# Two blocks in float32 on one core: a convolution's steps moved by one slot, a quarter of x turned before the first group

## The reference

```python
h = _rmsnorm(x, norm_pre_w[l])
proj = jnp.einsum('bsd,de->bse', h, w_in[l])
(q, k, v, o_g, z_a, i_pre, f_pre, u_b, z_b, g_a, g_b) = _partition(proj)
qk = jax.nn.silu(_causal_depthwise_conv(jnp.concatenate([q, k], axis=-1),
                                        qk_conv_w[l], qk_conv_b[l]))
```

## Time and profile before

| | us |
|---|---|
| three timed runs: lowest, median, highest | 1443.83, 1444.13, 1444.65 |
| profiled execution, its own time | 1438.61 |
| its span, first to last instruction | 1436.9 |
| PE busy in the span | 1424.9 |
| DVE busy | 879.3 |
| ACT busy | 702.4 |
| mean granted clock of PE | 0.999 |

### The profile page before, as it was taken

One profiled execution on the slowest core, in us unless ns is written; L12 is line 12 of the kernel. 1 busy time (PEld: TensorE's weight loads), 2 busy tenths in 40 slices (PEclk: granted clock), 3 DMA queues, 4 the chain that ended last, 5 costly groups with the idle time before them and its releaser, 6 DMA issues.

```text
span 1436.9 us, 27127 instructions
## 1 busy us (share of the span) xinstructions
PE 1424.9 (99%) x10514; PEld 1347.1 (94%) x10514; DVE 879.3 (61%) x1071; ACT 702.4 (49%) x925; POOL 67.7 (5%) x99
## 2 busy tenths in 40 slices
PE   8999999999999999999999999999999999999997
PEld 8999988899999999999999999888999998888886
DVE  5778774546766777546464655557555545667754
ACT  6555545445555433434334444436433345777643
POOL 1000000001010100000000000001000002211000
PEclk9999999999999999999999999999999999999999
DMA  7565555655556556565666666756655554334653
GB/s 273 188 208 179 195 182 178 208 181 179 160 176 197 181 173 193 173 198 183 204 193 193 195 194 222 246 180 219 201 169 174 176 179 130 117 118 149 220 194 126
DMA packets 72658, 265.98 MB, mean 185 GB/s; under 512 B 8168, under 2 KB 8432, under 8 KB 71664
## 3 DMA queue, kind: packets, MB, share of 16 engines
q1 hardware_dynamic: 70704, 253.38, 54.6%
q0 software_dynamic: 1440, 10.63, 2.0%
q10 hardware_dynamic: 432, 0.79, 0.2%
HBM read 260.56 MB, written 4.20 MB: 184 GB/s over the span
## 4 chain that ended last, share of the span: by engine, by line
PE 97%; DMA 1%; issue 0%; DVE 0%; SPq 0%; ACT 0%; POOL 0%; ACTq 0%; POOLq 0%; DVEq 0%
PE ps L370 21%; PE ps L374 21%; PE ps L372 21%; PE ps L362 9%; PE ps L364 9%; PE ps L363 9%; PE ps L489 2%; PE ps L792 1%; PE ps L581 1%; PE ps L592 1%; DMA raw<-in_w_stream 1%; PE ps L630 0%; PE ps L798 0%; PE ps L796 0%; SPq L463 0%
## 5 line engine op out<-in xcount | busy, mean ns | idle before, releaser
L1271 DVE TENSOR_TENSOR wl<-raw,wh 128x1024 fp32r<-128x1024 f32 x474 | 580.5, 1231 | 482.6 <-ACT wh L957 470.7
L957 ACT ACTIVATE wh<-raw 128x1024 fp32r<-128x1024 f32 x474 | 497.8, 1058 | 521.4 <-PE ps L374 376.0
L370 PE MATMUL ps<-xh,wh 128*128 128x256 f32 x1568 | 436.0, 278 | 0.5 <-DVE xl L1280 0.3
L372 PE MATMUL ps<-xl,wh 128*128 128x256 f32 x1568 | 434.0, 277 | 0.0
L374 PE MATMUL ps<-xh,wl 128*128 128x256 f32 x1568 | 434.0, 277 | 0.0
L370 PEld LDWEIGHTS ps<-xh,wh 128*128 128x128 f32 x1568 | 294.5, 188 | 1.2 <-DVE xl L1280 0.9
L372 PEld LDWEIGHTS ps<-xl,wh 128*128 128x128 f32 x1568 | 294.7, 188 | 0.1
L374 PEld LDWEIGHTS ps<-xh,wl 128*128 128x128 f32 x1568 | 294.6, 188 | 0.0
L370 PE MATMUL ps<-x2h,wh 128*128 128x272 f32 (+1 forms) x432 | 123.8, 287 | 0.0
L374 PE MATMUL ps<-x2h,wl 128*128 128x272 f32 (+1 forms) x432 | 123.3, 286 | 0.0
L372 PE MATMUL ps<-x2l,wh 128*128 128x272 f32 (+1 forms) x432 | 122.9, 285 | 0.0
(11 more groups left out here) (370 smaller groups left out, 2292.1 us busy)
## 6 DMA issues: line engine op xcount, KB each, us to landing
raw<-in_w_stream SPq DMA_DIRECT2D x474, 512.0 KB, 4.1
xr<-in_x POOLq DMA_DIRECT2D x1, 2048.0 KB, 13.1
x_kept<-xr POOLq DMA_DIRECT2D x1, 2048.0 KB, 8.1
x1r<-x_kept POOLq DMA_DIRECT2D x1, 2048.0 KB, 9.5
xn<-in_x SPq DMA_DIRECT2D x7, 256.0 KB, 7.1
out<-yn SPq DMA_DIRECT2D x6, 256.0 KB, 3.5
mrow<-bound_rows POOLq DMA_DIRECT2D x8, 128.0 KB, 3.6
poolw<-in_pool_w POOLq DMA_DIRECT2D x1, 1024.0 KB, 5.2
```

Of the source, the lines that this page charges most:

```text
L370: pe.matmul(out_at(j), whr[:, c, f], hi(kc)[:, tokens], start=st, stop=False, skip_group_check=True)
L372: pe.matmul(out_at(j), whr[:, c, f], lo(kc)[:, tokens], start=False, stop=False, skip_group_check=True)
L957: act.activation(slot_view(wh_at[r], layout), raw[r][:, :, :], ACT.Copy).then_inc(wh_done, 1)
L1271: tt(slot_view(wl_at[r], layout), raw[r][:, :, :], slot_view(wh_at[r], layout).bitcast(F32), ALU.subtract).then_inc(split_done, 1)
```

## The change

In the evacuation of queries and keys, ACT's bias and first tap move from k = 0 to 1 and its sigmoid from 4 to 5. DVE's three taps move from k = 1, 2, 3 to 2, 3, 4 and the product from 5 to 6. DVE's scaling out of the banks stays at k = 0. So at k = 0 and 1 the splits now stand ahead of what was ahead of them.

At the start, TensorE issues 8 warming transposes in place of 16 and then the turn of the second quarter, before slot 0. The third and fourth quarters are turned ahead of slots 1 and 2, in place of slots 2 and 3. ACT and DVE make the high and low parts of the second quarter between the splits of slots 1 and 2, and those of the third and fourth at k = 1 and 2. The second of ACT's four parts of squares moves from k = 2 to k = 1.

```diff
--- before.py
+++ after.py
@@ -515,7 +515,8 @@
 
         warm(18)
         x_turn(0)
-        warm(16)
+        warm(8)
+        x_turn(1)
 
         def groups(name, i, moving, token_kinds=(), before=None):
 
@@ -538,9 +539,9 @@
         XQ, XM = (headed(xqh, xh), headed(xql, xl)), (headed(xmh, xh), headed(xml, xl))
 
         def x_there(j, kind, k):
-            if j == 0 and k in (1, 2, 3):
+            if j == 0 and k in (1, 2):
                 pe.wait_ge(s_x_low, 2)
-                x_turn(k)
+                x_turn(k + 1)
             if j == 1 and k == 0:
                 pe.wait_ge(s_r0_diagonal, 1)
                 pe.wait_ge(s_const, 16)
@@ -981,6 +982,7 @@
         split(0, 0, LAYOUTS[0])
         x_high_parts(0)
         split(1, 1, LAYOUTS[1])
+        x_high_parts(1)
         split(2, 2, LAYOUTS[2])
 
         def out_squares(q, m):
@@ -998,7 +1000,7 @@
         def evac(kind, k, i, j, done):
             if kind == "qk":
                 q = i * 2 + j
-                if k == 0:
+                if k == 1:
                     act.wait_ge(psum_free[j], FIRST_G["QK"] // 2 + i + 1)
                     wait(act, s_qk, q)
                     if isinstance(i, int):
@@ -1009,7 +1011,7 @@
                             bias=small[:, bass.ds(SMALL["conv_b"][0] + q * 4 + jj, 1)],
                             scale=small[:, bass.ds(SMALL["conv_w"][0] + q * 16 + 4 * jj + 3, 1)])
                     last.then_inc(s_conv_first, 1)
-                if k == 4:
+                if k == 5:
                     act.wait_ge(s_conv, q + 1)
                     act.activation(work[1][:, :, :], work[0][:, :, :], ACT.Sigmoid).then_inc(s_conv_sigmoid, 1)
             if kind == "v" and k == 0:
@@ -1143,9 +1145,9 @@
 
         def attend(kind, k, i, j):
             if kind == "qk" and isinstance(i, int) and j == 0:
-                if k in (1, 2, 3):
-                    x_high_parts(k)
-                for n in ((0,), (), (1,), (2,), (3,), (), (), ())[k]:
+                if k in (1, 2):
+                    x_high_parts(k + 1)
+                for n in ((0,), (1,), (), (2,), (3,), (), (), ())[k]:
                     x_squares(n % 2, n // 2)
             if kind == "cq" and k in (1, 2):
                 x2_high_parts(k + 1)
@@ -1299,6 +1301,7 @@
         split(0, 0, LAYOUTS[0])
         x_low_parts(0)
         split(1, 1, LAYOUTS[1])
+        x_low_parts(1)
         split(2, 2, LAYOUTS[2])
 
         def split_high_low(hi, lo, src, s):
@@ -1322,19 +1325,19 @@
                         dve.tensor_copy(r0row[:, :], ps[:, 7, 0:S])
                         drain()
                     tt(work[1][:, :, :], banks(j), r0_over(4), ALU.mult).then_inc(psum_free[j], 1)
-                if k in (1, 2, 3):
-                    if k == 1:
+                if k in (2, 3, 4):
+                    if k == 2:
                         dve.wait_ge(s_conv_first, q + 1)
-                    sh = k
+                    sh = k - 1
                     for jj in range(4):
                         stt(out=work[0][:, jj, sh:S], in0=work[1][:, jj, 0:S - sh],
                                    scalar=small[:, bass.ds(SMALL["conv_w"][0] + q * 16 + 4 * jj + 3 - sh, 1)],
                                    in1=work[0][:, jj, sh:S], op0=ALU.mult, op1=ALU.add)
-                    if k == 3:
+                    if k == 4:
                         dve.drain().then_inc(s_conv, 1)
                     else:
                         drain()
-                if k == 5:
+                if k == 6:
                     dve.wait_ge(s_conv_sigmoid, q + 1)
                     tt(qk[:, bass.ds(q * 4, 4), :], work[0][:, :, :], work[1][:, :, :], ALU.mult).then_inc(s_qk, 1)
                     drain()
@@ -1558,8 +1561,8 @@
 
         def attend(kind, k, i, j):
             if kind == "qk" and isinstance(i, int) and j == 0:
-                if k in (1, 2, 3):
-                    x_low_parts(k)
+                if k in (1, 2):
+                    x_low_parts(k + 1)
                 if k == 4:
                     x_mean()
                 if k == 5:
```

## The result

| | us |
|---|---|
| before, median of 5 (lowest, highest) | 1444.06 (1443.70, 1444.65) |
| changed, median of 5 (lowest, highest) | 1436.77 (1436.76, 1437.47) |
| ratio, 95% interval | 0.995 (0.9939 to 0.9961) |
| changed, profiled execution and its span | 1437.47, 1435.7 |

The change gains 7.3 us, 0.5%, where I had forecast 1.4 and a range down to 1440.5. The profiled executions differ by 1438.61 - 1437.47 = 1.1 us only. So what was gained stands mostly between the profiled execution of before and its timed ones, the 5.5 us that I had set down as the same for both kernels.

What follows compares the result with a forecast made beforehand. TensorE, busy 1424.9 of 1436.9 us, was taken as the bound. Terms of -0.59 and -0.79, all others 0, gave -1.38 us from 1444.13, so 1442.8 us, with a range of 1440.5 to 1444.7.

Steps and rivals of the forecast that it cites:

- Start of slot 0, ACT and DVE at the start: First group: slot 0 still starts at 11.05, and the moved ACT and DVE work fits idle time or reserve, costing nothing.
- Slots 1 to 3, -1.38 us: First group: slot 3 begins 1.38 us earlier, from 0.59 us of waiting and one turn of 0.79 removed.
- Slots 4 to 7, nothing: First group: splits of slots 4 and 5 still arrive 0.8 and 0.9 us ahead of TensorE, so no cost.
- I take it as the same for both kernels: Whole kernel: the timed median's 5.5 us above the profiled time was assumed equal before and after the change.
- rival 3: Convolution's groups: timed runs wait for a late fourth split, so the change gains up to 5.5 us more, 1437.2; chance 9%.
- The convolution, "nothing": Eight groups of queries and keys: moving the convolution one slot later gives larger reserve but 0 us, as TensorE doesn't wait.
- the reserve of 1.3 us: Group of the loop before the change: fourth split ends at 161.71, TensorE wants it at 163.0.
- rival 2: First group: its matmuls get faster, for a gain of 2.3 us in all, 1441.8; chance 6%.
- The formula of the Trainium skill: Matmul of 256 columns: columns / 2.4 + 2.5, estimated 109 ns against the trace's 113 to 118; not used in the sum.
- The timeline's 0.34 us: First group, slot 2 at 19.11: the bracketed wait of TensorE, said to understate a loss of 0.59 us.

Runs made afterwards that it cites:

- e3: Kernel before with only the convolution moved one slot later, x turned as before: 1438.31 us, ratio 0.9976.
- e4: Kernel before with the convolution one slot later in its first group alone: 1438.37 us, ratio 0.9969.
- e1: Kernel before, unchanged, traced and timed again: three executions from 1438.2 to 1439.0 us, seven from 1443.7 to 1444.2.
- e5: Kernel before with the convolution one slot later in all groups but the first: 1443.86 us, ratio 0.999.
- e10: Changed kernel plus idle DVE arithmetic ahead of slot 15's split, and the loop reading all of x from xh and xl: 1438.42 us.
- e8: Kernel before with the loop over queries and keys reading all of x from xh and xl: 1440.54 us, ratio 0.9983.
- e9: Changed kernel with the fourth quarter of x turned directly behind the third, ahead of slot 1: 1436.81 us.

## Why the prediction was wrong

I had put the time at 1442.8 us and the range from 1440.5 to 1444.7; it is 1436.8. What the change saves in the first group was right. The sum failed at what it took to stay: the 5.5 us between the profiled and the timed runs, and the zero for the convolution.

- *Start of slot 0, ACT and DVE at the start:* right. Slot 0 waits for the low parts of x and not for a turn, and the added work fits the idle time.
- *Slots 1 to 3, -1.38 us:* right. From slot 0 to slot 3 the changed kernel takes 10.38 us where before took 11.78, 1.40 less, and to slot 8 it takes 24.75 where before took 26.24, 1.49 less. In times it stands at 1436.8 against 1438.3 and 1438.4 of e3 and e4, and against 1438.6, the median of before's 21 lower executions. Part of the 1.8 us to the last is what before loses at slots 13 and 14 (0.23 us in its trace), for which the sum had no term.
- *Slots 4 to 7, nothing:* right, no wait. The reserve was smaller than the 0.8 and 0.9 us forecast: the splits of slots 4 and 5 end 0.4 and 0.5 us ahead of the slots' first matmuls.
- *"I take it as the same for both kernels"*, of the 5.5 us between the profiled and the timed runs of before: **this step failed.** Before has two levels 5.4 us apart, and the trace was of the lower, while all five timed executions were of the upper. The changed kernel has only the lower, so the 5.5 us went with the change. I had the number in hand and no row for it, and gave it 9% as rival 3. That the measured gain is 7.3 us has some luck in it: about three executions of before in four are on the upper level, so that the median of five falls on the lower one about once in ten times (an estimate from 62 of 83), and the gain would then have been about 1.8 us, near the forecast.
- *The convolution, "nothing":* this failed with it, in two ways. First, the reserve of 1.3 us was read from a group of the loop and taken for all eight. The written-out group is not like them: DVE comes to it 2.6 us behind TensorE (the scaling at 39.88, TensorE's slot 8 at 37.29), and its splits of slots 13 and 14 end as TensorE comes to them (51.19 for 51.32, 54.11 for 54.06). The convolution's move turns the second into 52.07 - 48.33 = 3.7 us in hand in the changed kernel:

```profile
47.10 1.23 DVE L1273 TENSOR_TENSOR wl<-raw,wh 128x1024 fp32r<-128x1024 f32 x1
...
57.71 1.22 DVE L1327 TENSOR_TENSOR work<-ps,r0row 128x1024 f32<-128x1024 f32 x1 [0.34 <-PE ps L374]
58.87 1.23 DVE L1273 TENSOR_TENSOR wl<-raw,wh 128x1024 fp32r<-128x1024 f32 x1
```

  (47.10 is the split of slot 14, and it ends at 48.33; 57.71 and 58.87, the scaling of the next group and the split behind it, show that DVE now waits for TensorE and not for ACT.) Second, I priced a wait at its length. A meeting that holds TensorE by 0.03 us or less (slot 13 in e1) costs 5.4 us where the step changes with it ahead of the loop. In the sum's terms: the convolution's 0 is about -5.4 for each execution of before that is on the upper level, and about -0.3 for the others.
- *Rival 3* had the stretch and nearly the size (up to -5.5) and the wrong mechanism: a late fourth split in seven or eight groups. e4 and e5 show that the seven others don't matter. The argument against it was that all timed runs would have to be hit alike. They were, five of five, though only about three executions of four are: a step that is kept through the loop costs each of them the same.
- *"Matmuls of the first group get faster"* (rival 2) did not come about; the step there is 117.8 ns in every trace. The formula of the Trainium skill (TensorE: Matmul & The Clock Gate, Back-to-back issue gap), an estimate of 109 ns for 256 columns, is met by neither step. That section gives it for a matmul by itself and says that in a stream of weight loads and matmuls both set the spacing.
- *The timeline's 0.34 us* at slot 2 was told as the only wait of TensorE on a split or a low part. It is the only one that the table lists for line 370; the table for the whole span also has 0.3 us on a low part in the second block, and the holds at slots 13 and 14 stand in no table.
- *The second block:* the sum had no term for it. Both traces of the changed kernel lose 0.7 to 1.0 us there, with the wait at line 700.

## What to carry to other kernels

A profile is one execution. Where its time doesn't lie within the timed runs, look for a second level before anything is worked out, by tracing the same kernel again and comparing the distance of two matmuls' starts stage by stage. When an engine that bounds the kernel meets a producer within some 0.2 us, in any one group, a written-out first one above all, give that place a reserve: what the meeting costs is set by what the engine does behind it, and not by the wait.

## What was not expected of the hardware

TensorE ran the same matmuls (128 x 256, float32 in three passes, one weight load each) in one of two steps, 113.3 or 117.8 ns, with the granted clock at 1.00 in both. The step was kept over six groups and 130 us, and it changed only at a wait or at the meeting of a split and its matmul, at a place where the moving operand's addresses change, or within the first slots of a group that reads x with its first four chunks 4 elements further apart. That reading the first four chunks at the other addresses brings the faster step back is shown for the groups of the loop (e10's trace; e8 and e10: no upper level in 20 executions), and the same is seen at slot 10 in every trace. Whether it is the 4 elements or the place of the copies was not taken apart. Why slots 2 to 7 of the first group don't come back stays open: e9 took away the turn between and changed nothing. Why a meeting changes the step in one execution and not in another was not shown. What in the engine makes the two steps was not tried; nor was how the chance depends on the length of the wait.
